# Dense expert weights loaded in pairs of units, 8 KB a partition in one transfer, with gather tables of their own

## The reference, cut to what matters

```python
cand_i = (top_i[:, :, 0, :, None] * N_KEYS + top_i[:, :, 1, None, :])
best_s, best_pos = lax.top_k(cand_s, PEER_TOPK)
idx = jnp.take_along_axis(cand_i, best_pos, axis=-1)
g = jax.nn.softmax(best_s, axis=-1)
u_sel = expert_u[idx]
act = jax.nn.gelu(jnp.einsum('phkd,pd->phk', u_sel, xb), approximate=False)
coef = (g * act.astype(jnp.float32)).astype(xb.dtype)
return jnp.einsum('phk,phkd->pd', coef, expert_v[idx])
```

## Time and profile before

| | before |
|---|---|
| median of 3 runs | 1972.75 us (1969.97 to 1973.94) |
| the profiled execution's own time | 1973.12 us |
| its span in the profile | 1971.4 us |
| busy share of the span: PE, DVE, POOL, ACT | 93%, 80%, 53%, 36% |
| granted TensorE clock, mean | 0.961 of full |
| moved by DMA | 440 MB, 223 GB/s over the span |

### The profile page before, as it was taken

The page is one execution under the profiler, slowest core; times in us unless marked ns, Lnnn a source line. Parts: engine busy times, 40 slices in busy tenths (PEclk is TensorE's granted clock), DMA queues, the critical chain, the costliest instruction groups (busy, mean ns, idle before and its releaser), DMA issues.

```text
span 1971.4 us, 28772 instructions
## 1 busy us (share of the span) xinstructions
PE 1835.6 (93%) x10239; PEld 1584.9 (80%) x10239; DVE 1579.6 (80%) x2571; ACT 703.5 (36%) x1121; POOL 1046.6 (53%) x649
## 2 busy tenths in 40 slices
PE   6998869999999999999999999999999998988885
PEld 4776747999999899999978887878887676766764
DVE  5975867968989798888489999999997968757656
ACT  2342232433333344444333333333333433224441
POOL 1332225478888655565567666666764552344001
PEclk7998879999999999999999999999999999999888
DMA  8241332489999879988899999999995121200011
GB/s 346 88 166 59 131 147 75 134 300 314 312 315 305 279 262 317 312 294 306 305 361 352 356 352 354 355 353 350 364 355 202 57 96 54 75 22 3 1 56 51
DMA packets 159917, 440.47 MB, mean 223 GB/s; under 512 B 13648, under 2 KB 62928, under 8 KB 156752
## 3 DMA queue, kind: packets, MB, share of 16 engines
q1 hardware_dynamic: 64400, 254.71, 36.9%
q0 software_dynamic: 36864, 134.23, 18.2%
q10 hardware_dynamic: 58560, 50.34, 7.8%
HBM read 386.80 MB, written 52.43 MB: 223 GB/s over the span
## 4 chain that ended last, share of the span: by engine, by line
PE 70%; DVE 15%; issue 5%; POOL 4%; ACT 3%; DMA 2%; ACTq 0%; DVEq 0%; SPq 0%; PEldq 0%; POOLq 0%
PE PS L940 33%; PE PS L1147 25%; PE PS L1110 4%; POOL w_lo L832 3%; DVE arena L1784 1%; DVE arena L1975 1%; PE PS L1182 1%; ACT w_hi L1361 1%; PE PS L955 1%; DVE arena L1743 1%; PE PS L1173 1%; POOL arena L881 1%; PE PS L994 1%; DMA xres<-in_x 1%; DMA arena<-in_expert_u_rows,arena 1%
## 5 line engine op out<-in xcount | busy, mean ns | idle before, releaser
L832 POOL TENSOR_TENSOR w_lo<-raw,w_hi 128x1024 fp32r<-128x1024 f32 x300 | 723.8, 2413 | 795.0 <-ACT w_hi L1361 749.8
L1361 ACT ACTIVATE w_hi<-raw 128x1024 fp32r<-128x1024 f32 x332 | 351.9, 1060 | 989.3 <-PE PS L940 631.2
L940 PE MATMUL PS<-act_hi,w_hi 128*128 128x384 f32 (+1 forms) x1632 | 602.9, 369 | 29.7 <-DVE act_lo L1756 14.7
L940 PE MATMUL PS<-act_hi,w_lo 128*128 128x384 f32 (+1 forms) x1632 | 586.6, 359 | 0.0
L940 PE MATMUL PS<-act_lo,w_hi 128*128 128x384 f32 (+1 forms) x1632 | 586.3, 359 | 0.0
L940 PEld LDWEIGHTS PS<-act_hi,w_hi 128*128 128x128 f32 x1632 | 311.4, 191 | 78.7 <-issue 21.8
L940 PEld LDWEIGHTS PS<-act_lo,w_hi 128*128 128x128 f32 x1632 | 311.2, 191 | 25.7
L940 PEld LDWEIGHTS PS<-act_hi,w_lo 128*128 128x128 f32 x1632 | 311.9, 191 | 24.2 <-issue 1.4
L1147 PE MATMUL PS<-w_hi,act_hi 128*128 128x512 f32 x768 | 301.3, 392 | 5.5 <-ACT arena L1505 2.9
L1147 PE MATMUL PS<-w_lo,act_hi 128*128 128x512 f32 x768 | 300.1, 391 | 0.0
L1147 PE MATMUL PS<-w_hi,act_lo 128*128 128x512 f32 x768 | 300.0, 391 | 0.0
(11 more groups left out here) (330 smaller groups left out, 1901.9 us busy)
## 6 DMA issues: line engine op xcount, KB each, us to landing
raw<-in_expert_u SPq DMA_DIRECT2D x128, 512.0 KB
raw<-in_expert_v SPq DMA_DIRECT2D x128, 512.0 KB
raw<-in_w_in SPq DMA_DIRECT2D x52, 512.0 KB
arena<-in_w_ada SPq DMA_DIRECT2D x24, 1024.0 KB, 6.7
gel_d<-arena ACTq DMA_DIRECT2D x64, 384.0 KB
gates_d<-arena ACTq DMA_DIRECT2D x12, 2048.0 KB
arena<-gates_d SPq DMA_DIRECT2D x32, 768.0 KB, 7.2
arena<-gel_d SPq DMA_DIRECT2D x32, 768.0 KB
```

Of the source, the lines that this page charges most:

```text
L832: pool.tensor_tensor(w_lo[:, k % SPLIT, :], raw[:, k % RAW, :], w_hi[:, k % SPLIT, :].bitcast(F32), ALU.subtract).then_inc(lo_split, 1)
L940: mm = pe.matmul(PS[:, bank, 0:n_tok], w[:, k % SPLIT, c * P:(c + 1) * P], x[:, c, 0:n_tok], start=(i == 0 and n == 0), stop=(i == KC - 1 ...
L1361: act.activation(w_hi[:, k % SPLIT, :], raw[:, k % RAW, :], ACT.Copy).then_inc(hi_split, 1)
```

## The change

Two neighbouring units of U, or of V, come in one transfer of 128 x 2048 numbers, 8 KB a partition, 1.05 MB, into two neighbouring slots. Pairs fill slots 0 and 1 or 2 and 3, so the transfer of units u and u + 1 waits until `lower` of unit u - 3 is done. Only `raw_in` of the even slot counts the landing, and ACT waits on it for both units (`landing`). Units of other weights are loaded singly as before. In HBM the two tables are laid out by pairs; the gathers of V rows read a table of their own, `expert_v_rows`, which is a second copy of the same rows (the U gathers had their own table before).

```diff
+        def landing(u, k):
+            if u < U_EU:
+                return raw_in[k % RAW], 16 * (u // RAW + 1)
+            if u < U_IN2:
+                return raw_in[k % RAW // 2 * 2], 16 * (u // RAW + 1)
+            return raw_in[k % RAW], 16 * (u // RAW + 1 - (k % 2) * 2 * N_KEYS // RAW)
...
-            def expert_u(first, r):
-                for k in range(RAW):
-                    sp_.wait_ge(lo_split, r * RAW + (U_EU + first + k - RAW + 1))
-                    sp_.dma_start(raw[:, k, :], A["expert_u"][bass.ds(r * RAW + (first + k), 1)].rearrange(
+            def two_slots(k):
+                return raw[:, k:k + 2, :].rearrange("p a n -> p (a n)")
+
+            with sp_.Fori(0, N_KEYS // RAW) as r:
+                for k in range(0, RAW, 2):
+                    sp_.wait_ge(lo_split, r * RAW + (U_EU + k + 1 - RAW + 1))
+                    sp_.dma_start(two_slots(k), A["expert_u"][bass.ds(r * 2 + k // 2, 1)].rearrange(
                         "a p n -> (a p) n")).then_inc(raw_in[k], 16)
...
+            def two_values(u, i):
+                for n in range(2):
+                    sp_.wait_ge(*lowered(u + n - RAW))
+                sp_.dma_start(two_slots(u % RAW), A["expert_v"][i]).then_inc(raw_in[u % RAW], 16)
+
             quad(0, 0)
-            for k in range(2):
-                unit(U_EV + k, A["expert_v"][k])
+            two_values(U_EV, 0)
             quad(1, 1)
-            for k in range(2, RAW):
-                unit(U_EV + k, A["expert_v"][k])
+            two_values(U_EV + 2, 1)
...
             with sp_.Fori(0, NQ // 2 - 1) as r:
                 for b in range(2):
-                    for k in range(QUAD):
-                        if k < 3:
-                            sp_.wait_ge(lo_split, r * 6 + (U_EV + 3 * b + k + 1))
-                        else:
+                    for k in range(0, QUAD, 2):
+                        sp_.wait_ge(lo_split, r * 6 + (U_EV + 3 * b + (2 if k == 0 else 3)))
+                        if k:
                             sp_.wait_ge(dve_lo, r * 2 + (b + 1))
-                        sp_.dma_start(raw[:, k, :], A["expert_v"][bass.ds(r * 8 + (4 * b + k + 4), 1)].rearrange(
+                        sp_.dma_start(two_slots(k), A["expert_v"][bass.ds(r * 4 + (2 * b + k // 2 + 2), 1)].rearrange(
                             "a p n -> (a p) n")).then_inc(raw_in[k], 16)
...
-                table = A["expert_u_rows"] if s < SLOTS else A["expert_v"].rearrange("j i n -> (j i) n")
+                table = A["expert_u_rows"] if s < SLOTS else A["expert_v_rows"]
...
-                if r is None:
-                    act.wait_ge(raw_in[k % RAW], 16 * (u // RAW + 1))
-                else:
-                    act.wait_ge(raw_in[k % RAW], r * (16 // RAW) + 16 * (u // RAW + 1))
+                came, count = landing(u, k)
+                act.wait_ge(came, count if r is None else r * (16 // RAW) + count)
```

More of the change, by code:

```diff
@@ L749, in quad @@
                               else gel_d[i].rearrange("p c n -> p (c n)")).then_inc(eq_in[b], 16)
-            def expert_u(first, r):
-                for k in range(RAW):
-                    sp_.wait_ge(lo_split, r * RAW + (U_EU + first + k - RAW + 1))
-                    sp_.dma_start(raw[:, k, :], A["expert_u"][bass.ds(r * RAW + (first + k), 1)].rearrange(
+            def two_slots(k):
[4 more added lines that the diff above has]
+                    sp_.dma_start(two_slots(k), A["expert_u"][bass.ds(r * 2 + k // 2, 1)].rearrange(
                         "a p n -> (a p) n")).then_inc(raw_in[k], 16)
-            with sp_.Fori(0, N_KEYS // RAW) as r:
-                expert_u(0, r)
             for b in range(2):
@@ L782, in _ @@
                     quad(bass.ds(r * 2 + (b + 2), 1), b)
-            for k in range(QUAD):
-                unit(U_EV + N_KEYS - QUAD + k, A["expert_v"][N_KEYS - QUAD + k])
+            for k in range(0, QUAD, 2):
+                two_values(U_EV + N_KEYS - QUAD + k, (N_KEYS - QUAD + k) // 2)
             for w in range(32):
@@ L2485 @@
         "keys": a["sub_keys"][0].transpose(1, 3, 0, 2),
-        "expert_u": a["expert_u"][0].reshape(N_KEYS, N_KEYS, KC, P).transpose(1, 3, 2, 0).reshape(N_KEYS, P, D),
-        "expert_v": a["expert_v"][0].reshape(N_KEYS, N_KEYS, D).transpose(1, 0, 2),
+        "expert_u": a["expert_u"][0].reshape(N_KEYS, N_KEYS, KC, P).transpose(1, 3, 2, 0).reshape(
+            N_KEYS // 2, 2, P, D).transpose(0, 2, 1, 3).reshape(N_KEYS // 2, P, 2 * D),
+        "expert_v": a["expert_v"][0].reshape(N_KEYS, N_KEYS // 2, 2, D).transpose(1, 0, 2, 3).reshape(N_KEYS // 2, P, 2 * D),
+        "expert_v_rows": a["expert_v"][0].reshape(N_KEYS, N_KEYS, D).transpose(1, 0, 2).reshape(-1, D),
         "expert_u_rows": a["expert_u"][0].reshape(N_KEYS, N_KEYS, D).transpose(1, 0, 2).reshape(-1, D),
```

## The result

The changed kernel takes 1979.26 us (median of 8 runs, 1977.29 to 1982.36) against 1971.38 us for the kernel before (8 runs, 1967.22 to 1975.92). The ratio of the runs is 1.0044, 95% interval 1.0032 to 1.0055, which makes 8.7 us slower; the two medians lie 7.9 us apart. The profiled execution of the changed kernel took 1978.23 us, its span is 1976.5 us, 5.1 us more than before.

What follows compares the result with a forecast made beforehand. TensorE, 98.5 to 99.5% busy in both expert stages, was taken as the bound, so only the border counted: 1.1 + 1.8 = 2.9 us on 1972.75 us gave 1975.7 us, range 1970.5 to 1986 us.

Steps and rivals of the forecast that it cites:

- border forecast: Loads at the U/V border land later and V starts later: 1974.0 to 1979.6 us, chance 0.55.
- (B): U's first part and V: shorter lead fails, a fifth of some 100 pairs 0.5 us late; 1985.7 us, chance 0.17.
- (C): Gathers in the U stage: larger packets crowd them out, +3.6 us, with the border 1979.3 us; chance 0.08.
- Term (a): Border: last two U units load beside the last gate store, which lands 1.1 us later (0 to 1.5).
- Term (b): Border: V's unit 0 lands only with unit 1, 1.8 us later (1.3 to 2.6).
- The sum 2.9 us: Border: later store landing, 1.1 us, plus later unit 0, 1.8 us; bounds 1.3 and 6.9 us.
- longer slow stretch of the clock: After TensorE's pause at the border: same slow stretch expected, up to 2.8 us more as upper bound.
- The lead in the stages: U and V stages: pairs have less time between issue and use, but it suffices; cost 0 us.
- one gather beside it: V stage: 0.52 MB of gather beside 1.17 MB of loads, 1.7 MB in all, taking 4.8 us at 354 GB/s.
- the margin of 3.5 us: V stage: the pair for slots 0 and 1 lands by 1317.8 us, some 3.5 us before needed.
- With the quad behind it and not ahead: no tighter.: V stage: pair for slots 2 and 3, issued at 1304.78 and needed at 1313.22 us, has no less room.
- (D): Denser rows cut DMA time per unit by 12%: 1967 us at best, more likely 1972; chance 0.20.

Runs made afterwards that it cites:

- v_pairs: Pairs for V units alone with the gathers' own table, U units single, against the kernel before: ratio 1.0044, V stage 534.7 us.
- late_singles: Kernel before, but both loads of a pair start when the second slot is free, as two 4 KB-row transfers with own semaphores: ratio 1.0018.
- quad_first: Changed kernel with each quad issued ahead of the pair for slots 2 and 3 in the V loop: 2051.5 us, ratio 1.0407 to the kernel before.
- late_joint: Kernel before with paired loads started together as two 4 KB-row transfers, ACT waiting for both landings, in U and V: ratio 1.0044.

## Why the prediction was right or wrong

**The forecast and the range.** 1975.7 us was forecast, within 0.2% of before; measured are 1979.26 us and +0.4%, clear of 0.2% on the slow side. The range of 1970.5 to 1986 holds it. The likeliest case was the same time, with 0.52; the slower side had 0.42, of which 0.17 was the upper part of the border forecast and 0.25 the rivals (B) and (C). That 1979.26 also lies in the border forecast, 1974.0 to 1979.6, is luck: the kernel before came out 1.4 us lower in 8 runs than in the 3 of the forecast, and the loss of 8.7 us is above that forecast's upper bound of 6.9. Half of the loss stood in a place where the forecast had 0.

**Where TensorE stands still.** That the border is the place where the chain runs through weight transfers was right. ACT's wait there grew, all work behind it moved, and the V stage gave nothing back.

**Term (a), the gate store.** Forecast +1.1 us with a bound of 1.5. Measured from the copy of U unit 122 to SP's first quad: 19.49 us before, 21.37 with the change, 21.46 with U pairs alone, 19.62 with V pairs alone: +1.9 us. The bytes beside the store were right (1.05 MB on queue 1 and not 0.52), and so was their engine time: 23.3% of 12.4 us against 14.0% of 10.5 us, 1.4 us more. The step that failed is the 0.4 us of idle time that was taken off. None of it was used: the idle time went from 0.45 to 0.7 us, and the store's own packets took 8.8 us and not 8.6.

**Term (b), unit 0 with unit 1.** Forecast +1.8 us. Measured alone (v_pairs), from SP's quad to ACT's copy of unit 0: 11.60 us against 10.05 and 9.79 in the two profiles of before, so 1.6 to 1.8 us. Right.

**The sum 2.9 us,** measured 5.1. Beside (a), a term was missing: what others put into the queues while SP is late. With U pairs alone, ACT's copy of unit 0 came 4.4 us later, 2.0 from the store and 2.4 from gathers and a gelu store that had been behind it before. The upper bound of 6.9 us held for the border. Of it 2.8 us were reserved for a longer slow stretch of the clock, which did not come: the pause rose from 2.87 to 7.82 us, and the matmuls at 0.43 us were over 4.8 us after the first one (987.95 to 992.71), where they were after 6.1 us before. The second profiles have 3.0 us before and 3.1 us with the change, so the length scatters in both kernels.

**The lead in the stages, taken at 0.** Right for U: 597.2 and 596.9 us against 597.5 and 597.6. Wrong for V, 4.8 us. Its working had "one gather beside it". In the round in which a pair came 0.7 us late the changed kernel shows, from 1360.5 us, when the pair had just been issued, to 1369.7, when ACT copied it, on the queues (packets, MB, share of 16 engines)

```profile
q0 software_dynamic: 445, 1.65, 48.4%
q1 hardware_dynamic: 226, 1.44, 45.6%
```

and its copy in the timeline:

```profile
1369.72 1.06 ACT L1370 ACTIVATE w_hi<-raw 128x1024 fp32r<-128x1024 f32 x1 [3.34 <-DMA raw<-in_expert_v]
```

Queue 1 had 1.44 MB to bring (the pair and the quad's last 0.39 MB), more than the 1.17 MB of the round that I had worked out, and beside it stood not one gather but three (1.65 MB on queue 0). POOL starts a second gather after some units, and at the end of this stretch, from 1365 us on, the gathers had two thirds of the engines:

```profile
q0 software_dynamic: 300, 1.12, 66.8%
q1 hardware_dynamic: 79, 0.52, 26.8%
```

So the step that failed here is the one gather counted beside the pair. The lead alone was rightly taken at 0, since late_singles has the same lead and loses nothing in V; the joint landing and the larger rows, on top of it, had no price of their own in the forecast and cost about 2.6 and 3.1 us. One round that looks well is not the stage: the margin of 3.5 us was read from an easy one, and a slack that differs from round to round has to be taken at its worst.

**"With the quad behind it and not ahead: no tighter."** Right for the pair, as quad_first shows the other way round. But nobody asked who waits for the quad: DVE needs its gelus some 11 us after their issue (issued at 1353.51, used at 1365.13 after a wait of 0.35 us), and no row of mine had that lead. It cost seven waits, 3.9 us of DVE's time.

**Rival (B),** the lead doesn't hold, had the place half right and the size too high: 11 late pairs in V, 3.1 us in all, where it had a fifth of 100 pairs in both stages at 0.5 us. In U ACT's copy waited for a load three times (9.5 us with what ACT idles anyway, the longest 3.5; once in the second profile) and TensorE lost nothing. Chances were given to (B) and to the border alone as if it were one or the other; what came was the border and a smaller (B). Its cause is narrower than I gave it: late_singles has the same lead and no late unit. A unit that may be copied as soon as it is there hides what a pair, there only as a whole, does not.

**Rival (C),** crowded gathers, did not happen to the gathers: DVE's waits for them went from 39.7 to 34.1 us (36.4 to 35.8 in the second profiles) and TensorE's for POOL from 10.8 to 9.9 us. Its mechanism is seen at the border, where 8 KB rows moved 2.28 MB and 4 KB rows 2.02 MB in 10 us at like counts of packets. The Trainium skill, "DMA: Bandwidth & Descriptors", section "Queues, rings and completion order", has each engine go round its queues packet by packet, from which (C) followed with twice as large packets. The page's packet is a group of descriptors, some 9 to 17, and no run shows whether the packets that the profile counts are these. The trace agrees at the border (374 packets to 359), and not in the stretch above, in which the gathers had 300 packets and 66.8% of the engines, and queue 1 had 79 and 26.8%. Whether queue 1 had work on every engine all that time no view shows, so equal turns can't be taken for granted over some us.

**Rival (D),** denser rows pay: queue 1 took 35.7% of the engines where it took 36.9% (page, before; 36.0% and 37.7% in the second profiles). That is 3 and 4% of what it took; the loads of U and V are about half of its bytes. But most of it isn't the larger rows. By the packet records of the traces a 4 KB row in the U stage of weights took 196 and 199 ns before, an 8 KB row 368 and 371 ns, which is 184 and 186 ns for 4 KB; and with 4 KB rows that are merely loaded later, in late_singles and late_joint, it was 185 and 188 ns. In V the three are 188 and 191, 184 and 183, and 186 and 185 ns. So the row size by itself is worth 0 to 2%, and not the 12% of rows 9, which had compared a stretch with nothing beside it (with rows of 8 and 4 KB, and not 8 and 2) with one that was shared. What the later loading saved on the weights it added to the gathers, whose packets in U took 178 and 179 ns before, 188 and 190 ns in the two late kernels and 187 and 185 ns in the changed one. No stage became shorter. The same page's rule of at least 1 MiB a DMA, section "Rules for kernel authors", was followed here and the kernel is 0.44% slower: what cost TensorE time was when a load could be used.

## What to carry to other kernels

A larger transfer gives up two things that a profile of busy times doesn't show: the lead of its first part, and the landing of its first part by itself. Where the consumer takes the parts one by one from a ring of few slots, read from the trace how long before its use each part is there, in the worst round and not in a typical one, and take off one part's time and the other part's bytes. Before moving a transfer later, list what other engines issue on their own clock meanwhile, for it will be ahead of it; and look at stage boundaries first, where queues are full and the chain has no slack.

## What the runs showed of the hardware that I had not expected

- Two transfers of 0.52 MB with 4 KB rows, started together, served the V stage better than one of 1.05 MB with 8 KB rows: 529.2 us with separate landings, 532.1 and 532.2 with a joint one, 533.5 to 536.9 as one transfer. At the border one transfer was there sooner than both of two: 40.9 and 40.7 us against 42.5, and 37.5 against 38.7.
- 8 KB rows took 184 and 186 ns of engine time for each 4 KB in the U stage, and 4 KB rows that were loaded as late took 185 and 188 ns. The same 4 KB rows took 196 and 199 ns when loaded earlier: when a load ran changed its engine time more than the size of its rows did.
- The time at half clock after TensorE's pause did not follow the pause. It was 5.9 and 2.9 us in two profiles of the kernel before (pauses of 2.87 and 2.66 us) and 4.6 and 3.0 us with the change (7.82 and 7.67 us).
- A delay of 2.0 us in issuing a chain of loads became 4.4 us at its landing, while other queues went on issuing.
- Stretches in which two kernels are alike differ by up to 12 us between profiles (346.4 to 358.2 us to the fourth unit of U), more than the whole effect; stretches inside the expert stages of one kernel repeat within 1 us or so.
